# Opening with x laid out by features, LayerNorm whose variance ScalarE forms, and the last product's order of halves

## What is computed

```python
def layer_norm(x, g, b):
    xf = x.astype(jnp.float32)
    mu = xf.mean(-1, keepdims=True)
    var = jnp.square(xf - mu).mean(-1, keepdims=True)
    return ((xf - mu) * lax.rsqrt(var + LN_EPS)).astype(x.dtype) * g + b

def swiglu(x, w_in, w_out):
    gate, up = jnp.split(x @ w_in, 2, axis=-1)
    return (jax.nn.silu(gate) * up) @ w_out

    h = x
    for i in range(DEPTH):
        h = layer_norm(DN_ALPHA * h + 0.5 * swiglu(h, ffn_w_in[i, 0], ffn_w_out[i, 0]), ln_g[i, 0], ln_b[i, 0])
...
        h = jnp.square(jax.nn.relu(jnp.einsum('bsd,df->bsf', x, w_ff1[layer])))
        y = jnp.einsum('bsf,fd->bsd', h, w_ff2[layer])
        x = _layer_norm(DEEPNORM_ALPHA * x + y, ln2_g[layer], ln2_b[layer])
```

## Time and profile before

| | |
|---|---|
| median of 3 runs | 1522.58 us |
| the profiled execution's own time | 1522.43 us |
| its span, first to last instruction | 1520.6 us |
| TensorE matmul busy | 1512.0 us, 99% |
| DVE, ACT, POOL busy | 972.2, 761.6, 139.8 us |
| DMA | 283.71 MB, mean 187 GB/s |
| mean granted TensorE clock | 0.999 |

### The profile page before, as it was taken

How to read it: one execution, slowest core, us unless ns; L and a number is a source line. 1 busy time by engine, 2 the same in 40 slices (tenths; PEclk the granted TensorE clock), 3 DMA queues, 4 the chain that set the end, 5 groups by cost and what they waited for, 6 DMA issues and landing times.

```text
span 1520.6 us, 20606 instructions
## 1 busy us (share of the span) xinstructions
PE 1512.0 (99%) x8164; PEld 1300.5 (86%) x8164; DVE 972.2 (64%) x1013; ACT 761.6 (50%) x756; POOL 139.8 (9%) x141
## 2 busy tenths in 40 slices
PE   9999999999999999999999999999999999999998
PEld 8888889888888888888888888888898888888886
DVE  5556576765567556587667655557686556785555
ACT  5454465554545454454434545455536566354442
POOL 1000020100002000024021200002002200020000
PEclk9999999999999999999999999999999999999999
DMA  8554564355544654555544454556444434465551
GB/s 311 196 192 172 214 222 166 131 220 205 192 169 187 227 192 175 211 217 199 175 164 166 173 224 185 185 201 226 166 167 141 162 142 166 166 216 200 191 187 64
DMA packets 42264, 283.71 MB, mean 187 GB/s; under 512 B 5088, under 2 KB 5536, under 8 KB 9552
## 3 DMA queue, kind: packets, MB, share of 16 engines
q1 hardware_dynamic: 38016, 270.55, 48.3%
q0 software_dynamic: 2368, 8.59, 1.7%
q10 hardware_dynamic: 1808, 3.55, 0.6%
HBM read 281.55 MB, written 1.05 MB: 186 GB/s over the span
## 4 chain that ended last, share of the span: by engine, by line
PE 99%; DMA 0%; DVE 0%; ACT 0%; POOL 0%; issue 0%; SPq 0%; DVEq 0%; POOLq 0%; ACTq 0%
PE psum L1699 21%; PE psum L1594 16%; PE psum L1597 16%; PE psum L1598 16%; PE psum L1703 11%; PE psum L1726 5%; PE psum L1733 3%; PE psum L1639 2%; PE psum L1632 2%; PE psum L1626 2%; PE psum L1606 1%; PE psum L2125 0%; DMA weights_raw<-in_weights 0%; PE psum L2088 0%; PE psum L2146 0%; PE psum L1979 0%
## 5 line engine op out<-in xcount | busy, mean ns | idle before, releaser
L919 DVE TENSOR_TENSOR weights_lo<-weights_raw,weights_hi 128x2048 fp32r<-128x2048 f32 x247 | 569.7, 2318 | 318.2 <-ACT weights_hi L436 316.8
L436 ACT ACTIVATE weights_hi<-weights_raw 128x2048 fp32r<-128x2048 f32 (+1 forms) x254 | 479.5, 1890 | 301.2 <-PE psum L1598 144.3
L1699 PE MATMUL psum<-operand,weights_hi 128*128 128x512 f32 x1376 | 327.6, 390 | 0.0
L1699 PEld LDWEIGHTS psum<-operand,weights_hi 128*128 128x128 f32 x1376 | 255.3, 188 | 51.1
L1594 PE MATMUL psum<-weights_hi,hidden_hi 128*128 128x512 f32 x480 | 187.8, 391 | 0.0
L1597 PE MATMUL psum<-weights_lo,hidden_hi 128*128 128x512 f32 x480 | 187.6, 391 | 0.0
L1598 PE MATMUL psum<-weights_hi,hidden_lo 128*128 128x512 f32 x480 | 186.8, 389 | 0.0
L1703 PEld LDWEIGHTS psum<-operand,weights_lo 128*128 128x128 f32 x1376 | 176.4, 191 | 6.7
L1703 PE MATMUL psum<-operand,weights_lo 128*128 128x256 f32 x1376 | 178.5, 283 | 0.0
L1594 PE MATMUL psum<-weights_hi,operand 128*128 128x512 f32 x384 | 151.6, 395 | 0.0
L1597 PE MATMUL psum<-weights_lo,operand 128*128 128x512 f32 x384 | 149.9, 390 | 0.0
(11 more groups left out here) (299 smaller groups left out, 1844.4 us busy)
## 6 DMA issues: line engine op xcount, KB each, us to landing
weights_raw<-in_weights SPq DMA_DIRECT2D x254, 1024.0 KB, 4.8
ln_rows<-in_ln_rows POOLq DMA_DIRECT2D x16, 512.0 KB, 6.6
weights_raw<-in_weights SPq DMA_DIRECT2D x4, 512.0 KB, 6.6
normalised<-in_x SPq DMA_DIRECT2D x2, 512.0 KB, 6.2
ret_constants<-in_ret_constants ACTq DMA_DIRECT2D x1, 1024.0 KB, 7.7
out<-normalised SPq DMA_DIRECT2D x4, 256.0 KB, 2.0
gla_w_low<-in_gla_w_low ACTq DMA_DIRECT2D x1, 512.0 KB, 5.5
att_w_small<-in_att_w_small ACTq DMA_DIRECT2D x1, 512.0 KB, 5.6
```

The costliest lines, as they stand in the source:

```text
L436: nc.scalar.activation(w_hi[:, s, whole], raw[:, s, whole], ACT.Copy).then_inc(hi_split, 1)
L919: nc.vector.tensor_tensor(w_lo[:, s, :], raw[:, s, :], w_hi[:, s, :].bitcast(F32), ALU.subtract).then_inc(lo_split, 1)
L1699: mm(banks[b // 2][:, b % 2, :], w_hi[:, slot, cols], x_both[:, c, :, :].rearrange("p a t -> p (a t)"), start=c == 0, stop=False, skip_gro ...
```

## The change

It has four parts.

1. **The opening.** The host also hands over x by features (`x_turned`, four pieces of 128 partitions by 2 chunks by 256 tokens, 256 KB each). SP loads them into the tile `xn`, used as scratch, between quarters of tile 0 and halves of tile 1 (each contiguous in DRAM), then tile 2 and `ident`. ACT copies each piece to `x_hi`, DVE subtracts to `x_lo`. TensorE warms 8 times and does all 48 products, both token blocks of each chunk behind one another; the 16 transposes and 5 warming matmuls are gone.
2. **x by tokens** is loaded into `xn` later, by POOL, once `lo_split` stands at 8 (block 0) and 12 (block 1); the residual is made after that.
3. **LayerNorm.** `scaled_mean` gets a second column, epsilon's share is put in as a shift of the first (`mean_shift`), and `var` is formed on ACT: one ACTIVATE of 128x1, which waits for `surplus_ready`, writes `ln_rstd` and signals `var_ready`. POOL only raises to the power.
4. **The end.** In the eighth LayerNorm, DVE evacuates block 1's first half before it normalises block 0, and the last product does all of block 1's first half (12 matmuls) before its second.

The core of the diff:

```diff
@@block.sync
-            sp.dma_start(xn[:, 0, :], io["x"][0]).then_inc(x_loaded[0], 16)
-            for n in range(2):
-                for j in range(2):
-                    cols = slice(j * D, (j + 1) * D)
-                    sp.dma_start(raw[:, n, cols], io["weights"][n][:, cols]).then_inc(weight_loaded[n] if j else half_loaded[n], 16)
-            sp.dma_start(xn[:, 1, :], io["x"][1]).then_inc(x_loaded[1], 16)
+            load_chunks(0)
+            load_quarter(0)
+            load_quarter(1)
+            load_chunks(1)
+            load_quarter(2)
+            load_quarter(3)
+            load_chunks(2)
+            sp.dma_start(raw[:, 1, 0:D], second_tile[0]).then_inc(half_loaded, 16)
+            load_chunks(3)
+            sp.dma_start(raw[:, 1, D:], second_tile[1]).then_inc(weight_loaded[1], 16)
             sp.dma_start(raw[:, 2, :], io["weights"][2]).then_inc(weight_loaded[2], 16)
+            sp.dma_start(ident, io["constants"][:, 0, :]).then_inc(ident_loaded, 16)
@@block.gpsimd
-            def inverse_root(out, var, scale, eps, n, op=ALU.mult):
+            def inverse_root(out, n, var=None, scale=1.0, eps=0.0):
...
-                link(nc.gpsimd.tensor_scalar(out, var, scale, eps, op, ALU.add))
+                if var is not None:
+                    link(nc.gpsimd.tensor_scalar(out, var, scale, eps, ALU.mult, ALU.add))
                 nc.gpsimd.tensor_tensor(out, out, minus_half[:, 0:n], ALU.pow).then_inc(rstd_ready, 1)
...
-            pool.wait_ge(operand_ready, KC // 2)
+            pool.wait_ge(x_lo_done, KC // 2)
             for tb in range(TB):
+                pool.wait_ge(lo_split, 4 * tb + 8)
+                pool.dma_start(xn[:, tb, :], io["x"][tb]).then_inc(x_loaded[tb], 16)
+            for tb in range(TB):
+                pool.wait_ge(x_loaded[tb], 16)
                 residual(tb, ALPHA)
@@block.scalar, layer_norm
-                        link(nc.scalar.activation(squares[:, cols], xn[:, tb, cols], ACT.Square, bias=scaled_mean[:, tb:tb + 1],
+                        link(nc.scalar.activation(squares[:, cols], xn[:, tb, cols], ACT.Square, bias=scaled_mean[:, tb, b:b + 1],
                                                   scale=D ** -0.5, accum_out=moment[:, tb, b:b + 1]))
-                        act.sem_inc(var_ready if b else first_moment, 1)
+                        if b == 0:
+                            act.sem_inc(first_moment, 1)
+                    act.wait_ge(surplus_ready, 2 * (ln - 1) + tb + 1)
+                    nc.scalar.activation(ln_rstd[:, tb:tb + 1], moment[:, tb, 3:4], ACT.Identity, bias=moment[:, tb, 1:2],
+                                         scale=-1.0).then_inc(var_ready, 1)
@@block.vector, layer_norm
-                            nc.vector.tensor_scalar(scaled_mean[:, tb:tb + 1], row_sum[:, 2 * tb:2 * tb + 1], -2 * D ** -1.5, None,
-                                                    ALU.mult).then_inc(mean_ready, 1)
+                        nc.vector.scalar_tensor_tensor(
+                            out=scaled_mean[:, tb, :], in0=row_sum[:, 2 * tb:2 * tb + 1].to_broadcast([P, 2]), scalar=-2 * D ** -1.5,
+                            in1=mean_shift[:, :], op0=ALU.mult, op1=ALU.add).then_inc(mean_ready, 1)
...
+                    if ln == 8 and tb == 0:
+                        dve.wait_ge(resid_ready, 2 * ln)
+                        evacuate(1, 0)
                     count[0] += 1
                     dve.wait_ge(rstd_ready, count[0])
                     normalise(halves[0])
@@block.tensor, block_product
-                        if final is not None and s == tiles - 1:
-                            order.sort(key=lambda at: at[1])
+                    if final is not None:
+                        halves_from = 0 if final == 8 and tb else tiles - 1
+                        order.sort(key=lambda at: (min(at[0], halves_from), at[2] if at[0] >= halves_from else 0))
@@block.tensor, opening
+                def products(n, k, x, w, start=False, stop=False):
+                    for tb in range(TB):
+                        last = mm(out[:, tb, :], x[:, 4 * n + k, tb * P:(tb + 1) * P], w[:, n, k * NCOL:(k + 1) * NCOL],
+                                  start=start, stop=stop, skip_group_check=True)
...
-            turn_x1 = turn_rows("x", xn, 1, block_acc(1), x_loaded[1], lambda b: 16)
-            opening_unit(pairs[0], turn_rows("x", xn, 0, block_acc(0), x_loaded[0], lambda b: 16), turn_x1)
-            first_unit(N_FFN0, pairs[0], "x", turn_x1, blocks=(1,))
+            opening_unit(pairs[0])
             pe.wait_ge(ident_loaded, 16)
```

More of the change, by code:

```diff
@@ L201, in build @@
         warm_ready = sem("warm_ready")
-        half_loaded = [sem(f"half_loaded{n}") for n in range(2)]
+        chunks_loaded = [sem(f"chunks_loaded{g}") for g in range(KC // 2)]
+        quarter_loaded, half_loaded = [sem(f"quarter_loaded{k}") for k in range(3)], sem("half_loaded")
+        x_hi_done, x_lo_done = sem("x_hi_done"), sem("x_lo_done")
         first_hi, first_lo = sem("first_hi"), sem("first_lo")
@@ L1612, in turn_normed, with first_unit @@
                 return turn_rows(f"ln{ln}", xn, tb, block_acc(tb), xn_ready, lambda b: 4 * (ln - 1) + 2 * tb + b + 1)
-            def first_unit(n, out, what, turn_second, blocks=range(TB)):
-                for tb in blocks:
+            def first_unit(n, out, what, turn_second):
+                for tb in range(TB):
                     t = slice(tb * P, (tb + 1) * P)
@@ new lines, in block_product @@
+                    order = [(s, k, half) for s in range(tiles) for k in range(2) for half in range(2)]
+                    if final is not None:
+                        halves_from = 0 if final == 8 and tb else tiles - 1
+                        order.sort(key=lambda at: (min(at[0], halves_from), at[2] if at[0] >= halves_from else 0))
+                    for j, (s, k, half) in enumerate(order):
+                        slot = slot_of(n + s)
+                        if j == 0 or s > max(at[0] for at in order[:j]):
+                            pe.wait_ge(lo_split, n + s + 1)
+                            pe.wait_ge(ready, value(tb, s))
+                        h_hi, h_lo, c = chunks[2 * s + k]
+                        inner = (None, None)
+                        if (tb, s, k, half) in hooks:
+                            hooks[tb, s, k, half]()
+                        if final is not None and final < 8 and (tb, s, k, half) == ((1, 1, 1, 1) if tiles == 2 else (1, 2, 0, 0)):
+                            inner = turn_normed(final, 0)
+                        cols = slice(k * D + half * NCOL, k * D + (half + 1) * NCOL)
+                        last = three(acc[:, 2 * tb + half, :], h_hi[:, c, t], h_lo[:, c, t], w_hi[:, slot, cols],
+                                     w_lo[:, slot, cols], first and s == 0 and k == 0,
+                                     final is not None and s == tiles - 1 and k == 1, inner)
+                        if final is not None and s == tiles - 1 and k == 1 and (tb, half) != (1, 1):
+                            last.then_inc(acc_ready, 1)
+                        if tb == TB - 1 and s not in [at[0] for at in order[j + 1:]]:
@@ L1867, in lo_by_hi @@
-                    by_hi(n, k, x_lo, False)
+                    pe.wait_ge(x_lo_done, 2 * n + k // 2 + 1)
+                    products(n, k, x_lo, w_hi)
                 def hi_by_lo(n, k):
                     pe.wait_ge(first_lo if k < 3 else lo_split, 3 * n + k + 1 if k < 3 else n + 1)
-                    mm(out[:, 0, :], x_hi[:, 4 * n + k, 0:P], w_lo[:, n, k * NCOL:(k + 1) * NCOL], start=False,
-                       stop=(n, k) == (1, 3), skip_group_check=True)
-                for turn_bank in turn_first:
-                    turn_bank()
@@ L2333, in _weight_stream @@
     tiles = ffn(0, 0)
+    for n, parts in ((0, 4), (1, 2)):
+        tiles[n] = tiles[n].reshape(P, parts, TILE // parts).transpose(1, 0, 2).reshape(P, TILE)
     tiles += units(a["gla_w_in"][0], (D, D + NCOL, 0, NCOL, 2 * D, 2 * D + NCOL)) + _row_tiles(a["gla_w_out"][0])
```

153 lines of the change are left out of this document (74 added, 79 removed).

## The result

The changed kernel takes **1527.88 us** (median of 7 runs, 1527.34 to 1528.53); the kernel before took 1522.5 (7 runs, 1522.37 to 1522.61) beside it. The ratio is 1.0035, with a 95% interval of 1.0026 to 1.0045. It is slower by 5.4 us, where 3.9 of gain were forecast, and 7.4 above the range's upper end. The profiled execution took 1527.34, with a span of 1525.3 (before: 1522.43 and 1520.6).

The account below looks back on a forecast made before the run. TensorE, busy 99% of the span, was taken as the bound. Opening 3.0, LayerNorm 0.4 and end 0.5 sum to 3.9 us off 1522.43: 1518.5, or 1518.6 as a median; range 1517.0 to 1520.5.

Parts of the forecast that it names:

- The wider `scaled_mean` costs below 0.1 each, under TensorE's matmuls: LayerNorm on DVE: the two-column instruction costs below 0.1 us each, covered by TensorE's matmuls.
- Opening, 3.0 gained: Start: first product at 5.3, the ffn's first matmul at 16.8 instead of 19.83, 3.0 us gained.
- the third k of tile 0: Opening's supply: needed at 8.2, its loads there at 7.2, ACT's split 0.58 more, so 0.4 us to spare.
- x by tokens on POOL's queue, 0: Later load of x on POOL's queue: cost 0, covered by idle DMA; without that cover 1 MB costs 2.5 us.
- LayerNorm, 0.4 of 1.3: LayerNorms: shorter POOL chain lets the power start earlier, easing TensorE's waits; up to 1.3 us, 0.4 taken.
- the race: LayerNorm's second block: POOL's power starting ahead of DVE's split gives up to 1.3 us; behind it, nothing changes.
- End, 0.5: Kernel's end: last power ends at 1516.16 instead of 1516.67, held by DVE's centring; 0.5 us gained, 0.8 without a hold.
- A, the late clock: Rival, opening: TensorE's clock rises 3 us later than 6.5, 1.5 us lost, 1520.1; chance 0.12.
- B, the small loads coming late: Rival, opening: small loads land late; 1522.9 at half rate, 1530.5 if one behind another; chance 0.07.
- C: Rival: LayerNorm and end give nothing, the opening gives its 3.0 alone, 1519.6; chance 0.06.
- D: Upper side: powers win each race and the end too, 3.5 + 1.3 + 0.8, 1517.0; chance 0.75 together with the forecast.
- The case on the other side: The prediction's slower case, opening's small loads coming late: up to 1530.5; chance 0.03 past +0.2%.

Follow-up runs that it names:

- a_ts: Changed kernel with `scaled_mean` written by two one-input TENSOR_SCALAR, the shift as an immediate, instead of one two-input instruction: 1518.83 us.
- open_only: Kernel before with only the changed opening and the later load of x by tokens; LayerNorm and end as before: 1519.46 us.
- b_ln: Kernel before with only LayerNorm's arithmetic changed: variance on ACT, power alone on POOL, `scaled_mean` by two TENSOR_SCALAR: 1521.17 us.
- b_end: Kernel before with only the end changed: order of evacuations and of the last product: 1522.38 us.
- a_ts_oldend: `a_ts` with the end as in the kernel before: 1518.64 us.
- a_ts_warm: `a_ts` with 16 warming matmuls instead of 8: 1518.74 us.
- a_ts_hold: `a_ts` with 16 warming matmuls and the first product held until three quarters of tile 0 are split: 1520.98 us.
- a_half: Changed kernel with POOL's piece of the split 512 columns instead of 1024, DVE taking over the rest: 1521.62 us.

## Why the prediction was wrong

**The step that failed** is the sentence "The wider `scaled_mean` costs below 0.1 each, under TensorE's matmuls", and with it the rivals, none of which had it. I costed the instruction by its size, 128x2, and not by what it reads. It cost 1.64 to 1.69 in the places shown, in seven LayerNorms; its cover, the matmuls of the next unit, ran out each time, and 8.4 us reached the end. I named a cover for it, and no price for the case in which the cover is gone. With that one instruction written in another way (`a_ts`), the time is 1518.83 where 1518.6 was forecast.

The trace of before held the clue. In the same LayerNorm, DVE:

```profile
192.61 0.15 DVE L955 TENSOR_SCALAR scaled_mean<-row_sum 128x1 f32<-128x1 f32 x1
...
193.88 0.47 DVE L965 SCALAR_TENSOR_TENSOR moment<-moment 128x1 f32<-128x1 f32 x1
```

and POOL:

```profile
191.94 2.40 POOL L338 TENSOR_TENSOR weights_lo<-weights_raw,weights_hi 128x1024 fp32r<-128x1024 f32 x1 [4.89 <-ACT weights_hi L434]
```

POOL ends at 194.34. The one-input L955 ran for 0.15 in the middle of that. L965 has two columns of `moment` in SBUF as its tensors, takes 0.22 where POOL is idle, and took 0.47 here (0.48 to 0.49 in five more LayerNorms): it ended at 194.35, with POOL. An instruction of the form of L965 at the place of L955, at 192.61, would end at 194.35 too, 1.6 late: the loss could have been read from three rows.

The Trainium skill (SBUF — State Buffer, "SBUF: two separate sides") says that a DVE instruction with two SBUF inputs and a GpSimd instruction that reads SBUF lock each other out, that whichever starts first has the pair "for the whole instruction", and that the other waits. By that rule, the traces agree: 1.80 under a piece of 2.40, 0.27 under the end of one of 1.30, 0.155 to 0.157 with the second input in PSUM, under a piece of 2.40 too. I had used the rule for POOL's power at the end, where DVE is the one in possession, and not in the other direction, for the DVE instruction that the change brought.

Point by point:

- *Opening, 3.0 gained:* the number right, the path in part another, so the close fit is partly luck. 3.0 by the medians (`open_only`, 1522.47 to 1519.46), 3.05 and 3.35 in two profiles. In the five profiles with the opening's start as changed, the first product came at 4.90 to 5.23 instead of 5.3, and the ffn at 16.48 to 17.23, with 16.81 in the middle, where 16.8 was forecast. But the third k of tile 0, which I had with 0.4 to spare, was what the ffn's start followed: in four of the five, TensorE waited 0.21 to 0.88 for its split. The sum has the ffn follow the first product and TensorE's pace; that the quarter landed at the time that gives 16.8 is the luck.
- *x by tokens on POOL's queue, 0:* right; `open_only` has it and gains all of the 3.0.
- *LayerNorm, 0.4 of 1.3:* the mechanism was right, its size too small. In the six LayerNorms that have the race, `b_ln` wins it six times, by 0.07 to 0.10, and `a_ts` five times, by 0.09 to 0.11; in its seventh LayerNorm it loses by 0.05, and the power takes 1.05. ACT's instruction took 0.29, not 0.2, but POOL followed it by 0.08 (193.11 to 193.19), not 0.2, and in `b_ln`, with a second short instruction ahead of it, the split on DVE came 0.08 later than before (195.13 against 195.05). In the kernel as changed the race is not won once, since the hold makes ACT's sum late: in the place shown the power took 0.85 behind DVE's split.
- *End, 0.5:* the size was near (7.82 to 7.46, with spans to 0.1; 0.5 in `b_ln`), the attribution wrong. `b_end` gives nothing and `b_ln` 0.52: what counts is that POOL has one instruction behind the centring instead of two. The power ended 0.41 behind the centring; I had 0.43. The evacuation, foreseen 0.12 earlier by the new order, came 0.11 behind the last matmul's modelled end instead of 0.16: 0.05 earlier. With the old order and the variance on ACT (`b_ln`, `a_ts_oldend`) it comes 0.04 behind: block 0's power ends sooner, DVE is free in time, and the new order has nothing left to gain.
- *Rivals:* A, the late clock, is small: without any warming 0.8 are lost. B, the small loads coming late, did not happen: the first product came earlier than I had it, though it is a landing that sets the ffn's start. C lacked the cost that decided. D's 3.5 for the opening has no working behind it; the most that a profile shows is 3.35. The case on the other side should have been this one: its place and price were in the trace.

## What to carry to other kernels

Ask of each instruction that a change adds not only how large it is but where its inputs lie and what POOL does at that moment; here a DVE instruction of 128x1 with two inputs in SBUF stood for up to 1.85 us, and the whole LayerNorm chain with it. Look for an instruction of the same form under the same neighbour, in the trace of before: one that ends together with POOL's is the sign. Where a second input holds only a constant, give it as an immediate, or take an input from PSUM; and once a chain has slack of a few tenths only, try each part of a change by itself.

## What the runs showed of the hardware

- The hold comes even at the smallest size. The same 128x1 instruction took 0.16 alone and 1.846 at the longest under POOL's 2.40; it ended 0.01 to 0.02 after POOL's. With an input in PSUM it took 155 to 157 ns sixteen times, seven of them under POOL's 2.40. Halving POOL's piece brought the longest to 0.734. A second value that is an operand per partition and no tensor did not hold it: the TENSOR_SCALAR L962 of the kernel before takes both its values from `row_sum` in SBUF, and took 0.21 to 0.22 sixteen times, also at 193.51 under POOL's 2.40.
- An ACTIVATE of 128x1 took 0.29 to 0.30 (sixteen times each in three profiles), and POOL started 0.08 after it.
- TensorE's pace rises at a time that differs between executions whose first TensorE instructions are the same. Stretches of 1 us of `a_ts_warm` and of `a_ts_hold`, from 4 us, both in the warming (columns: us, PE, PEld, DVE, ACT, POOL, PEclk, DMA share, GB/s):

```profile
4.00:5.00 1.00, 1.00 (x10) 1.00 (x10) 0.92 (x2) 0.68 (x2) 0.00 (x0) 1.00 0.79 283
```

```profile
4.00:5.00 1.00, 1.00 (x6) 1.00 (x6) 1.00 (x2) 0.57 (x1) 0.00 (x0) 1.00 0.96 313
```

Ten records in the one, six in the other, with two records to a matmul. They follow each other by 0.21 at first and by 0.11 later; the pace rises at 4.2 in `a_ts_warm` and at 5.4 in `a_ts_hold`. These two ran on different chips, but `open_only` and `a_half` ran on the same one, and their first four products took 1.16 from 5.04 and 1.69 from 5.23. The granted clock reads 1.00 in all of these stretches, so at the start of these executions it does not show which of the two levels TensorE has, and the pace of like matmuls must be read instead.
